# Two of three token groups with 64 stationary columns in the experts that have three groups

## The reference, cut to what matters

```
for e in range(N_EXPERTS):                       # 8, EXPERT_FF = 3584
    he = silu(t @ w1[e]) * (t @ w3[e])           # w1, w3: 1024 x 3584
    out = out + gates[:, e:e + 1] * (he @ w2[e]) # w2: 3584 x 1024
```

## Time and profile before

| | |
|---|---|
| median of three runs | 1203.07 us (1202.67 to 1203.28) |
| span of the profiled execution, first to last instruction | 1200.8 us |
| the profiled execution's own time | not given apart from its span; the median of the three runs is 2.3 us above that span |
| PE busy | 1171.2 us, 98% |
| data read from memory | 417.45 MB, 349 GB/s over the span |

### The profile page before, as it was taken

One profiled execution on the slowest core, in us unless ns is written; L12 is line 12 of the kernel. 1 busy time (PEld: TensorE's weight loads), 2 busy tenths in 40 slices (PEclk: granted clock), 3 DMA queues, 4 the chain that ended last, 5 costly groups with the idle time before them and its releaser, 6 DMA issues.

```text
span 1200.8 us, 21122 instructions
## 1 busy us (share of the span) xinstructions
PE 1171.2 (98%) x9420; PEld 679.8 (57%) x9421; DVE 348.9 (29%) x605; ACT 262.8 (22%) x396; POOL 58.6 (5%) x114
## 2 busy tenths in 40 slices
PE   8999999999999999999999999999999799999998
PEld 8888888888997444434434434544443353444334
DVE  6977876666995101001001000100100010010000
ACT  5785344344781010000000000000000000000000
POOL 5401300000001000000000000000000000000000
PEclk9999999999999999999999999999999899999999
DMA  7559665564149999999999999999999999999995
GB/s 245 184 171 316 212 200 184 187 199 141 43 178 422 428 423 391 387 425 429 433 425 423 431 430 427 427 428 428 424 432 425 432 427 429 431 423 429 424 426 240
DMA packets 66351, 419.06 MB, mean 349 GB/s; under 512 B 4627, under 2 KB 39056, under 8 KB 50385
## 3 DMA queue, kind: packets, MB, share of 16 engines
q1 hardware_dynamic: 64240, 414.21, 84.9%
q0 software_dynamic: 2016, 3.46, 0.8%
HBM read 417.45 MB, written 2.10 MB: 349 GB/s over the span
## 4 chain that ended last, share of the span: by engine, by line
PE 87%; DMA 7%; ACT 2%; DVE 2%; issue 1%; POOL 0%; SPq 0%; DVEq 0%; ACTq 0%
PE ps L1387 23%; PE ps L1379 14%; PE ps L1469 12%; PE ps L1116 7%; DMA w_pair<-in_moe_w_dram 7%; PE ps L1493 7%; PE ps L833 5%; PE ps L835 5%; PE ps L834 5%; PE ps L1121 3%; PE ps L1415 1%; ACT expert_h L1954 1%; PE ps L1402 1%; PE ps L1361 1%; PE ps L1425 0%
## 5 line engine op out<-in xcount | busy, mean ns | idle before, releaser
L1387 PE MATMUL ps<-w_pair,expert_in 128*32 128x384 f32 (+1 forms) x2688 | 255.7, 539 | 3.9 <-DMA w_pair<-in_moe_w_dram 2.7
L1387 PEld LDWEIGHTS ps<-w_pair,expert_in 128*32 128x32 f32 x2688 | 100.1, 110 | 153.9 <-issue 147.0
L1379 PE MATMUL ps<-w_pair,expert_in 128*64 128x448 f32 x896 | 175.1, 547 | 4.6 <-DMA w_pair<-in_moe_w_dram 4.6
L1998 DVE TENSOR_TENSOR w_lo<-w_raw,w_hi 128x2048 fp32r<-128x2048 f32 (+2 forms) x63 | 127.5, 2050 | 35.7 <-ACT w_hi L1569 35.6
L1379 PEld LDWEIGHTS ps<-w_pair,expert_in 128*64 128x64 f32 x896 | 63.5, 138 | 111.0 <-issue 104.8
L1116 PE MATMUL ps<-act_both,w_hi 128*128 128x512 f32 x352 | 122.5, 396 | 0.0
L1469 PE MATMUL ps<-w_pair,expert_h 128*32 128x512 f32 (+1 forms) x1344 | 109.8, 486 | 0.9 <-ACT expert_h L1954 0.9
L1569 ACT ACTIVATE w_hi<-w_raw 128x2048 fp32r<-128x2048 f32 (+2 forms) x62 | 104.4, 1718 | 4.4 <-DMA w_raw<-in_mla_w_kvb_dram 2.4
L2582 DVE TENSOR_TENSOR expert_h<-expert_h,ps 128x896 f32<-128x896 f32 x20 | 21.8, 1088 | 275.1 <-PE ps L1379 140.1
L1121 PE MATMUL ps<-act_both,w_lo 128*128 128x256 f32 x352 | 91.3, 280 | 0.0
L1469 PEld LDWEIGHTS ps<-w_pair,expert_h 128*32 128x32 f32 x1344 | 47.5, 110 | 63.0 <-issue 51.8
(11 more groups left out here) (403 smaller groups left out, 1404.9 us busy)
## 6 DMA issues: line engine op xcount, KB each, us to landing
w_pair<-in_moe_w_dram SPq DMA_DIRECT2D x59, 3584.0 KB, 34.4
w_pair<-in_moe_w_dram SPq DMA_DIRECT2D x42, 1792.0 KB, 12.5
w_raw<-in_ffn_w_dram SPq DMA_DIRECT2D x33, 1024.0 KB, 5.5
w_ring<-in_moe_w_dram SPq DMA_DIRECT2D x16, 1792.0 KB
w_raw<-in_lru_w_in_dram SPq DMA_DIRECT2D x8, 1024.0 KB, 5.5
w_ring_low<-in_moe_w_dram SPq DMA_DIRECT2D x8, 896.0 KB
w_ring_high<-in_moe_w_dram SPq DMA_DIRECT2D x8, 896.0 KB
w_ring_high<-in_moe_w_dram SPq DMA_DIRECT2D x7, 1024.0 KB
```

The source lines that it names most:

```text
L1379: ins = pe.matmul(ps[s * WIDE:(s + 1) * WIDE, 2 * g + b, 0:WIDE_COLS], in_x[:, k, 0:WIDE], ring_cols(first_unit + k, (2 * s + g) * PART + ...
L1387: ins = pe.matmul(ps[j * STRIP:(j + 1) * STRIP, 2 * g + b, 0:wide], in_x[:, k, g * STRIP:(g + 1) * STRIP], ring_cols(first_unit + k, j * P ...
L1998: dve.tensor_tensor(w_lo[s][:, 0:w], raw[s][:, 0:w], w_hi[h][:, 0:w].bitcast(F32), ALU.subtract).then_inc(lo_ready, 1)
```

## The change

The 64-column form is used for groups 0 and 1 of every turn, and a third group keeps the 32-column form. The instructions of each turn with three groups change; those of turns with two groups stay the same. In `up` each unit of a three-group turn becomes 8 matmuls with 64 stationary columns and then 8 with 32. In `down` each block PAIR row becomes `wide_row`, and THIRD's rows stand between them as before. The semaphores of a unit are raised by the last group as before, so the split into halves of 256 columns isn't needed in three-group turns. ScalarE and VectorE read groups 0 and 1 in the layout that the wide form leaves.

```diff
-        def wide_of(n):
-            return groups_of(n) == 2
+        WIDE_GROUPS = 2
...
-                            if wide_of(n):
+                            if g < WIDE_GROUPS:
                                 for b in range(2):
                                     for s in range(2):
                                         ins = pe.matmul(ps[s * WIDE:(s + 1) * WIDE, 2 * g + b, 0:WIDE_COLS], in_x[:, k, 0:WIDE],
...
-                                        if g or k == KD - 1:
+                                        if g == many - 1 or k == KD - 1:
                                             ins.then_inc(strip_used[2 * b + s], 1)
...
-                            marked = r == RUN - 1 or r == MID_ROW - h
+                            marked = many == WIDE_GROUPS and (r == RUN - 1 or r == MID_ROW - h)
...
+                    thirds = many - WIDE_GROUPS
                     for strip in range(STRIPS):
+                        landed(M_W2 + 2 * strip)
+                        pe.wait_ge(hT_ready, g_base + 2)
+                        for r in range(MID_ROW):
+                            wide_row(r, strip)
+                        if thirds:
+                            pe.wait_ge(hT_ready, g_base + 3)
                             for r in range(MID_ROW):
                                 for j in range(STRIPS):
-                                    ins = block_product(block, r, strip, j, u)
+                                    ins = third_product(r, strip, j)
...
+                        landed(M_W2 + 2 * strip + 1)
+                        if thirds:
+                            wide_row(MID_ROW, strip)
                             for j in range(STRIPS):
+                                ins = third_product(MID_ROW, strip, j)
...
+                        for r in range(MID_ROW + thirds, RUN):
+                            wide_row(r, strip)
+                        if thirds:
                             for r in range(MID_ROW + 1, RUN):
                                 for j in range(STRIPS):
+                                    ins = third_product(r, strip, j)
...
-                    if wide_of(n):
+                    if g < WIDE_GROUPS:
                         act.activation(wide_rows(g), wide_sums(g), ACT.Silu).then_inc(silu_ready, 1)
...
-                    h, sums = (wide_rows(g), wide_sums(g)) if wide_of(n) else (e_h[:, g * PART:(g + 1) * PART], group_sums(g))
+                    h, sums = (wide_rows(g), wide_sums(g)) if g < WIDE_GROUPS else (e_h[:, g * PART:(g + 1) * PART], group_sums(g))
```

More of the change, by code:

```diff
@@ L1455, in down, with third_product @@
                 def down():
[L1457 to L1469, removed]
+                    def third_product(r, strip, j):
+                        u = M_W2 + 2 * strip + (r > MID_ROW - j // 2)
+                        a = 2 * PART + r * P + strip * STRIP
+                        c0 = r * D + j * DOWN_COLS - (u - M_W2) % 2 * HALF_RUN
+                        return pe.matmul(ps[j * STRIP:(j + 1) * STRIP, out_bank(n, THIRD), 0:DOWN_COLS], hT[:, a:a + STRIP],
+                                         ring_cols(u, c0, DOWN_COLS),
                                          start=strip == 0 and r == 0, stop=strip == STRIPS - 1 and r == RUN - 1,
@@ L1494, in wide_row @@
                                                 ring_cols(u, c0 + at, wide), start=strip == 0 and r == 0 and at == 0,
-                                                stop=strip == STRIPS - 1 and r == RUN - 1 and at > 0, tile_position=(0, h * WIDE))
+                                                stop=strip == STRIPS - 1 and r == RUN - 1 and at + wide == HALF_COLS, tile_position=(0, h * WIDE))
                                 if marked:
@@ L1501, in down @@
                     pe.wait_ge(token_ready, min(n + 2, E) if static else held(pe, n + 1))
-                    final = blocks_of(n) - 1
+                    thirds = many - WIDE_GROUPS
                     for strip in range(STRIPS):
-                        u = M_W2 + 2 * strip
-                        landed(u)
-                        if wide_of(n):
[L1507 to L1519, removed]
+                        landed(M_W2 + 2 * strip)
[4 more added lines that the diff above has]
+                            pe.wait_ge(hT_ready, g_base + 3)
@@ L1520, in down @@
                             for r in range(MID_ROW):
                                 for j in range(STRIPS):
-                                    ins = block_product(block, r, strip, j, u)
-                                    if j >= STRIPS // 2 and block == final and r == MID_ROW - 1:
+                                    ins = third_product(r, strip, j)
+                                    if j >= STRIPS // 2 and r == MID_ROW - 1:
                                         ins.then_inc(strip_used[j], 1)
-                        landed(u + 1)
@@ L1526, in down @@
-                        for block in range(blocks_of(n)):
+                        landed(M_W2 + 2 * strip + 1)
+                        if thirds:
+                            wide_row(MID_ROW, strip)
                             for j in range(STRIPS):
-                                ins = block_product(block, MID_ROW, strip, j, u if j < STRIPS // 2 else u + 1)
-                                if j < STRIPS // 2 and block == final:
+                                ins = third_product(MID_ROW, strip, j)
+                                if j < STRIPS // 2:
@@ L1530, in down @@
                                     ins.then_inc(strip_used[j], 1)
-                        for block in range(blocks_of(n)):
+                        for r in range(MID_ROW + thirds, RUN):
+                            if static and n == E - 1 and strip == STRIPS - 1 and r > MID_ROW + 1:
+                                pe.wait_ge(last_landed[r - MID_ROW - 2], 16)
+                            wide_row(r, strip)
+                        if thirds:
                             for r in range(MID_ROW + 1, RUN):
-                                if static and n == E - 1 and strip == STRIPS - 1 and r > MID_ROW + 1:
-                                    pe.wait_ge(last_landed[r - MID_ROW - 2], 16)
@@ L1535, in down @@
                                 for j in range(STRIPS):
-                                    ins = block_product(block, r, strip, j, u + 1)
-                                    if block == final and r == RUN - 1:
+                                    ins = third_product(r, strip, j)
+                                    if r == RUN - 1:
                                         ins.then_inc(strip_used[j], 1)
```

## The result

The changed kernel takes 1219.31 us (median of four, 1219.13 to 1220.19) against 1202.87 us (1202.67 to 1203.28). The ratio is 1.0138, with a 95% interval of 1.0126 to 1.0149: slower by 16.4 us. The forecast was 1223.8 us, within 1210 to 1230.

The account below looks back on a forecast made before the run. PE and weight transfers were both taken as near their limit, with PE alone setting the time after the change. Shape switches +32.5 us, less 11.8 of starving, made 1203.07 + 20.7 = 1223.8 us; eight in ten within 1210 and 1230.

Parts of the forecast that it names:

- Streaming costs the same in either form: Three-group turns: 184 fewer matmuls in each are worth 0, with bounds of -1 and +1 us over four turns.
- Each change of shape has a price: Three-group turns, up and down: 109 switches to 32 columns and 97 back add 32.5 us on PE.
- the 0.20 for a change back to 64 columns up: Units up, after 384-column rounds: 0.15 us gap plus 0.05 for slower first records, 60 times, 12.0 us.
- The pair of rows 9 (0.32): Turn 7: one switch out and one in take 0.32 us; times 103 gives 33, used to check the 32.5.
- The starving comes back in full: Turns 3, 5 and 6: PE's waits for weights and lower clock, 11.8 us, disappear under the added work.
- A pair of turns takes 205.9 us: A three-group plus a two-group turn on PE, against 205.8 us for its transfers, so the lead stops shrinking.
- The conversion to the median: Whole kernel: the median of the runs lies 2.3 us above the profile's span.
- Cheap switches: Rival, switches inside a unit: half the cost, as next weights load ahead while PE streams; 1207.6 us, 8%.
- a fixed price of 0.010 us for each record: Rival, all matmul records: paid on top of streaming, so fewer records give 14.7 us back; 1209.1 us, 3%.
- Starving that stays: Rival, turns 5 and 6: they still wait for weights, little of the 11.8 us returns; 1232.6 us, 7%.
- Not slower: Rival, before 1009 us: transfers are the bound and PE's addition fits under them; 1203, at best 1201 us, 5%.

Follow-up runs that it names:

- few-switches kernel: Changed kernel with the same 64- and 32-column matmuls of three-group turns in another order, changes of tile shape down from 206 to 69: 1206.57 us, ratio 1.0027.
- two small-matmul kernels: Kernel before plus 30 unused two-column matmuls between the 32-column groups of turn 6: 1213.18 us with 64 stationary columns, 1204.08 us with 32.
- the one with few changes up: Changed kernel, reordered for few changes of shape in the products up only: 1211.64 us, ratio 1.0065.

## Why the prediction was right, and where its sizes were off

- **Streaming costs the same in either form: right.** The few-switches kernel keeps the 64-column form and is within 3.4 us of the kernel before, and in the phases up nothing but 0.145 us for each change is left to explain.
- **Each change of shape has a price: right in kind, high in size.** 109 x 0.13 + 60 x 0.20 + 37 x 0.17 = 32.5 us were forecast, 29.7 measured, 0.144 for each of 206. The term too high is the 0.20 for a change back to 64 columns up. I had taken its 0.15 of gap from the one place at 460.73, where 128-column transposes follow; the row at 698.82 beside it has 0.11. In the changed kernel the gap is 0.12 at each of the 55 changes from 384-column rounds to 64-column tiles, and 0.12 before those transposes too. Why it was 0.03 longer there before stays open. The whole pair of switches costs 4.80 - 4.53 = 0.27 us, not 0.33. The pair of rows 9 (0.32), which seemed to confirm the sum, was one between 64 and 128 columns. With 0.15 for the change back up the sum is 29.5.
- **The starving comes back in full: right in the amount, wrong in the reason given.** I argued that PE's added work ahead of turn 6 fits under it. The 7.7 us of turn 0 don't, as the kernel with the change in turn 0 alone shows; only turns 2 and 4, where the ring has room, add to the lead. They add 15.0 us, which is more than 11.9, so the amount was covered all the same, and that was luck. Where they add less, as in the few-switches kernel and the one with few changes up, forecasts by that argument were too low (1205 for 1206.6, 1209 for 1211.6).
- **A pair of turns takes 205.9 us: 205.1 measured,** against 205.8 for its transfers, and nothing starves.
- **The conversion to the median.** I took 2.3 us between span and time; every execution lies 1.8 above its own span, and the one profiled before was not the median one. The remaining 1.2 us (17.6 by spans, 16.4 by medians) is the spread of single executions.
- **The rivals.** Cheap switches are excluded by the two small-matmul kernels (0.14 us for a change). These don't exclude a fixed price of 0.010 us for each record, since a small matmul of the same shape, two records, costs 0.06. Turn 2's phases up do: 256 records fewer would have given 2.6 us back, and the changes leave room for 0.1. Starving that stays is seen where turn 0 alone is made longer, not in the changed kernel. Not slower is excluded by the time.

No version that I ran beats the kernel before. Its three-group turns have no change of shape inside a unit, and the few-switches order only approaches it (+3.4 us).

## What to carry to other kernels

Before mixing tile shapes on TensorE, count the changes of shape on the path and price each at what the trace shows at its existing ones, between the same two shapes; when a shape has to change, put all work of one shape together and alternate the order of the halves, so that two neighbours share a shape. Where an engine sometimes starves for a prefetched stream, added work was free only in the stretch in which the buffer had room (1.1 us for 9.5 of work in turn 2); while it was full, a longer stage held the stream back by as much (11.3 us in turn 0). To price a change there, compare the bytes moved by the time at which the starving begins. Two forms with the same streamed columns, at 448 to 512 for each matmul, were worth the same here, whatever number of matmuls one of them saved.

## What the runs showed of the hardware

The gap was nearly the same for all pairs of shapes here: 0.10 us from 64 to 32 columns, 0.12 back, 0.10 between 64 and 128, with some places at 0.14 to 0.15 behind rounds of 256 or 384 columns, and then a first round slower by 0.03 us with 32 columns and 0.05 with 64. The Trainium skill says in TensorEngine Tiling (Array Packing), section Key Properties, that changing the tiling mode drains the engine; the runs agree and add the size. Not expected was that behind a stop of 2.14 us records ran at the lower clock level (4.91 us for what took 3.21, granted clock 0.72 from 1000 to 1006 us), so that a wait for weights can cost more than its length. It doesn't always: in the kernel before, the stop of 2.58 us that ended at 1000.01 left the clock at 1.00 (996 to 1012 us).
